# Starting the large on-chip buffers of a two-block transformer kernel at multiples of 128 bytes

## The chip, the cores and the metric

The kernel runs on one core of a Trainium2 chip. The metric is the device time of one execution in microseconds. Unless a sentence names the profiled execution, a time is the median over several executions.

## What is computed

The reference is two blocks, one after the other, on 256 tokens of width 1024, all in 32-bit floats.

```
first block (16 meta tokens are put ahead: 272 tokens)
    h = h + token_mixer(h)            # retention and mLSTM, both directions, 4 heads each
    h = h + expert_choice_ffn(h)      # 16 experts of width 2816, each takes its 34 best tokens
    h = rmsnorm(h)
second block, layers 0 and 1
    x = x + rmsnorm(mixer(rmsnorm(x)))          # layer 0: attention and convolution, layer 1: gated linear recurrence
    x = x + rmsnorm(cross_attention(x, memory)) # 256 memory rows
    x = x + rmsnorm(swiglu(rmsnorm(x)))         # width 2816
```

## The kernel before

Everything that stays on the chip lies in a handful of named buffers, allocated one behind the other in the order of the calls of `sb`, each 128 partitions by so many 32-bit columns:

- `weight_ring` (lines 148 ff., `W`), 22528 columns, takes the weights as they arrive from memory.
- `hT` is the stream, the running hidden state turned so that features lie on partitions. `squares` (`SQ`) is scratch of the same size.
- `arena` (`Z`), 25096 columns, is carved up by `z(...)` into the working tiles of each stage: the mixer's heads, the gathered tokens `xs` and hidden rows of the experts, the keys and values of the memory, and in the second block the normed input (`input_high`, `input_low`), the outputs of attention (`mixed_low`) and the hidden rows of the feed-forward layers (`hidden_high_a`, `hidden_high_b`).
- `rstd`, `vec_cols`, `gate_w`, `router_w` and `small` hold per-feature and per-token columns.

`rounded(name, over, at, cols)` (line 159) lays a second name over a part of a buffer, at `BASE[over] + 4 * at` bytes. It is how the tiles with names of their own come about: `weights_ring` over the first 20480 columns of `weight_ring`, `mixed_high` and `mixer_high_a` over the columns behind them, `hidden_low_b` over `hT`, and most others over `arena`.

The three long stages, in order of time:

1. The first mixer, to some 200 us.
2. The experts, from some 200 to 1500 us. Each of the 16 experts streams three weight matrices (gate, up, down: 2816 KB a transfer, four transfers a matrix) through eight slots of the ring. The tokens of an expert, 64 columns wide and held in the arena, are the stationary side of a matmul and the weights in the ring are the moving side (line 1250 for gate and up, line 1328 for down). Between them TensorE projects the memory rows to keys and values (line 1217), from weights which eight transfers of 2048 KB bring into the arena (line 588).
3. The second block, from some 1520 us. Its weights come in chunks of 1024 KB. ScalarE rounds each chunk to its high part (line 2141), VectorE takes the low part (line 2854), and a product is three passes: high times high, low times high, high times low (`three_passes`, and `token_part` for the first two chunks after a norm). For the input projections the stationary side is a piece of the weights and the moving side 256 columns of `input_high` or `input_low` (line 1369), except in `token_part` (line 1400), where the two change sides. For the output projections 512 columns of weights move and the stationary side is a 128-column piece of `mixed_high`, `mixed_low`, `hidden_high_a` and so on (also line 1369). Each of the two feed-forward layers has 22 input chunks of 48 matmuls.

The order of instructions on every engine is written out by hand and does not depend on where a buffer lies.

Of the kernel before, what the change touches and what calls it, by code (L numbers as in the profile page):

```python
# [22 lines left out]
KT = D // P  # L23
SEQ = 256
META = 16
T = META + SEQ
# [8 lines left out]
ARENA = 25096  # L35
# [91 lines left out]
def build(nc, t, out):  # L127

    with ExitStack() as ctx:
        BASE = {}  # L130

        def sb(name, cols, dt=F32):
            made = ctx.enter_context(nc.sbuf_tensor(name, [P, cols], dt))
            BASE[name] = nc.sbuf_base - 4 * cols
            return made
# [3 lines left out]
        def S(name):  # L139
            if name not in sems:  # L140
                sems[name] = ctx.enter_context(nc.semaphore(name))
            return sems[name]
# [2 lines left out]


        W = sb("weight_ring", SLOTS * SLOT)
        ident = sb("ident", P)
        ones = sb("ones", P)
        hT = sb("hT", KT * T)  # L150
        SQ = sb("squares", KT * T)
        RSTD = sb("rstd", T)
        VC = sb("vec_cols", 256)
        GW = sb("gate_w", KT * 16)
        RW = sb("router_w", KT * 16)
        small = sb("small", 192)
        Z = sb("arena", ARENA)

        def rounded(name, over, at, cols):

# [3 lines left out]
        def vec(name, i):  # L164
            tile, at, n = VEC_AT[name]
            return VC[:, tile * P + at + i:tile * P + at + i + 1]

        def vec_cols(name, n):
            tile, at, _ = VEC_AT[name]
            return VC[:, tile * P + at:tile * P + at + n]  # L170

        cursor = [0]

        def z(cols, at=None):
            if at is None:
                at = cursor[0]
                cursor[0] += cols
            assert at + cols <= ARENA, (at, cols)
            return Z[:, at:at + cols]

        def tiles(ap, n):
            return ap.rearrange("p (t n) -> p t n", t=n)
# [26 lines left out]
        mvT, moT, rkT, rqT, rvT, rgT = (z(H * T) for _ in range(6))  # L209
        rk_rq = Z[:, cursor[0] - 4 * H * T:cursor[0] - 2 * H * T]  # L210
        mv, rv = z(TT * 512), z(TT * 512)
        xtok = Z[:, cursor[0] - 2 * TT * 512:cursor[0]]
        DEC = z(H * TT * T)
        dist_fwd, dist_bwd = z(256 + T), z(256 + T)
        dist_both = Z[:, cursor[0] - 2 * (256 + T):cursor[0]]
        bar_fwd, bar_bwd = z(T), z(384)
# [25 lines left out]
        floors = tiles(QKP[:, 0:8 * T], 8)  # L242
        head_denom, head_square = SQ[:, 1632:1632 + T], SQ[:, 1632 + T:1632 + 2 * T]
        ret_squares = QKP[:, 0:H * T]
# [20 lines left out]
        mm = z(2 * KT * 256, 12288)  # L265
        mem_gains = VC[:, 192:208]
        utok = z(TT * D, 16384)
# [19 lines left out]
        logitsT, affW, picked, running, vals = (z(n, o + T * i) for i, n in enumerate((T, T, T, T, 40)))  # L287
        ys = SQ[:, 0:512]
        Se = SQ[:, 512:768]
        xs_tok = SQ[:, 768:1280]  # L290
        htok = hT[:, 0:2 * D]
# [16 lines left out]
        cu = hT[:, 1024:1024 + 4 * 258]  # L308
        fox_e = [SQ[:, 0:384], SQ[:, 384:768]]
        fox_pt = [SQ[:, 768:1152], SQ[:, 1152:1536]]  # L310
        frow, frow2, frow3 = YG[:, 0:256], YG[:, 256:512], YG[:, 512:768]
# [52 lines left out]
        def landed(s):  # L364
            return S(f"ring_landed{s}")
# [88 lines left out]
        def raw_slot(k):  # L454
            return W[:, (k % CSLOTS) * CSLOT:(k % CSLOTS) * CSLOT + SLOT]

        def second_half(k):
            return W[:, (k % CSLOTS) * CSLOT + SLOT:(k % CSLOTS + 1) * CSLOT]

# [56 lines left out]
        def _(sp):  # L516
# [7 lines left out]
            def stab_load(n):  # L524
                r = 4 * (n % 2) + n // 2
                sp.dma_start(stabs(n), unit_rows[r:r + 1].to_broadcast([P, T]))                  .then_inc(S("stab_landed" if n < 3 else "late_stab_landed"), 16)

            for k, (name, c) in enumerate(A_CHUNKS):
# [21 lines left out]
                if k == 15:  # L550
                    sp.wait_ge(S("pool_mixer"), H * TT)
                    sp.wait_ge(S("rot_out"), 2 * H)
                    for n in range(3, 8):
                        stab_load(n)
            sp.dma_start(tiles(RW[:], KT), t["w_router"][0].rearrange("(t p) n -> p t n", p=P))\
              .then_inc(S("router_w_landed"), 16)
# [7 lines left out]
            def expert_slot(s):  # L564
                return W[:, s * DFF:(s + 1) * DFF]

# [5 lines left out]
            def pair_slot(g):  # L572
                return W[:, 2 * g * DFF:2 * (g + 1) * DFF]

# [15 lines left out]
            def last_down_load():  # L590
# [3 lines left out]
                mid = (ESLOTS - 1) * DFF  # L594
                sp.dma_start(W[:, 2 * g * DFF:mid], src[:, 2 * g * DFF:mid]).then_inc(landed(g), 16)
                sp.dma_start(W[:, mid:LAST_ROWS], src[:, mid:LAST_ROWS]).then_inc(landed(ESLOTS - 1), 16)
                sp.dma_start(W[:, LAST_ROWS:FT * D], src[:, LAST_ROWS:FT * D]).then_inc(S("apart_landed"), 16)
# [201 lines left out]
        def _(pe):  # L799
# [282 lines left out]
            def router(group):  # L1082
# [3 lines left out]
                for i in group:  # L1086
                    g = i % 4
                    at = EXP * (i - 1 if g == 3 else i)
                    last = pe.matmul(bank[4][32 * g:32 * g + 32, 0:T], RW[:, at:at + 2 * EXP], stream3[:, i, :],
                                     start=(i < 4), stop=(i >= 4), skip_group_check=True)  # L1090
# [644 lines left out]
        def _(act):  # L1735
            steps = [0]

            def after(ins):

                steps[0] += 1  # L1740
                ins.then_inc(S("act_step"), 1)
                act.wait_ge(S("act_step"), steps[0])
# [295 lines left out]
            for e in range(EXP):  # L2038
# [6 lines left out]
                if e == 0:  # L2045
                    act.wait_ge(S("hidT_ready"), 1)
                    take_slots(0)
                    act.wait_ge(S("norm_sum"), 2)
                    after(act.activation(RSTD[:, 0:256], bank[7][:, 0:256], ACT.Ln, bias=eps, scale=1.0 / D))
                    act.activation(RSTD[:, 0:256], RSTD[:, 0:256], ACT.Exp, scale=-0.5).then_inc(S("norm_rstd"), 1)  # L2050
                if e + 1 < EXP:
# [368 lines left out]
        def _(dve):  # L2420
            steps = [0]

            def after(ins):

                steps[0] += 1
                ins.then_inc(S("dve_step"), 1)
                dve.wait_ge(S("dve_step"), steps[0])
# [34 lines left out]
            for j, n in enumerate(VEC_COUNT):  # L2462
                last = dve.tensor_copy(VC[:, P * j:P * j + n], bank[7][:, T + P * j:T + P * j + n])
            last.then_inc(S("small_ready"), 1)
# [17 lines left out]
            dve.memset(qkp[:, :, PAD + T:2 * PAD + T], 0.0).then_inc(S("small_ready"), 1)  # L2482
            dve.tensor_scalar(half_a, VC[:, B_A_AT:B_A_AT + 8], 0.5, None, ALU.mult)
            dve.tensor_scalar(half_i, VC[:, B_A_AT + 8:B_A_AT + 16], 0.5, None, ALU.mult).then_inc(S("small_ready"), 1)
            lam = VC[:, LAM_AT:LAM_AT + 8]
# [231 lines left out]
            gains = vec_cols("ffn_norm_g", KT).rearrange("p (t a) -> p t a", a=1).to_broadcast([P, KT, 16])  # L2717
            dve.tensor_tensor(tiles(RW[:], KT), tiles(RW[:], KT), gains, ALU.mult).then_inc(S("router_gain"), 1)
            after(dve.tensor_tensor(logit_rows, ident[:, 0:EXP], ident[:, 32:32 + EXP], ALU.add))
# [94 lines left out]
            for e in range(EXP):  # L2814
# [14 lines left out]
                if e == 0:  # L2829
                    dve.wait_ge(S("norm_rstd"), 1)  # L2830
                    m_T = tiles(mT, KT)
                    for L in range(2):
                        normed = tiles(mm[:, 2048 * L:2048 * L + 2048], KT)
                        for i in range(KT):
                            dve.scalar_tensor_tensor(out=normed[:, i, :], in0=m_T[:, i, :], scalar=mem_gains[:, 8 * L + i:8 * L + i + 1],
                                                     in1=RSTD[:, 0:256], op0=ALU.mult, op1=ALU.mult).then_inc(S("norm_out"), 1)
                dve.wait_ge(S("up_used"), 8 * e + 8)
# [439 lines left out]
```

## Time and profile before

| | |
|---|---|
| median of 3 executions | 2224.63 us (2223.53 to 2227.73) |
| the profiled execution | 2228.88 us, of which the span of instructions is 2227.1 us |
| granted TensorE clock, mean | 0.987 |
| TensorE matmul busy | 2106.0 us (95%) |
| TensorE weight load busy | 1307.8 us (59%) |
| VectorE busy | 770.7 us (35%) |
| ScalarE busy | 634.4 us (28%) |
| moved by DMA | 725.21 MB |

A matmul is issued before the one ahead of it has drained, so the busy time of TensorE counts overlapping intervals once, and the duration of one matmul is longer than the distance between two. Where the rate of TensorE matters, the distance between the starts of two groups in the timeline is what counts.

### The profile page before, as it was taken

How to read it: one execution, taken by the hardware profiler on the slowest of the kernel's cores; microseconds unless marked ns; L12 is line 12 of the kernel's file. 1: busy time of each engine (PE TensorE's matmuls, PEld its weight loads, DVE VectorE, ACT ScalarE, POOL GpSimd, SP SyncE). 2: the span in 40 equal slices, each digit the busy share in tenths (PEclk: the TensorE clock that was granted, in tenths of full speed). 3: DMA queues.
4: the chain of work that ended last, by engine and by line, in shares of the span. 5: the costliest groups of instructions: out<-in, count | busy, mean ns of one | idle time of the engine just before them, and what ended most of it. 6: DMA issues, size and time to landing. Idle time of an engine off the chain costs nothing.

```text
span 2227.1 us, 27225 instructions
## 1 busy us (share of the span) xinstructions
PE 2106.0 (95%) x12048; PEld 1307.8 (59%) x12048; DVE 770.7 (35%) x1105; ACT 634.4 (28%) x1008; POOL 43.2 (2%) x74
## 2 busy tenths in 40 slices
PE   9999999899898999899889889989999999999999
PEld 9987443333333443333333333427888998988997
DVE  8983211011010111011011011116765564876553
ACT  6664100000000000000000000005565444865442
POOL 3201000000000000000000000000000000000000
PEclk9999999999999999999999999999999999999999
DMA  8529999999999999999999999997444656544553
GB/s 238 173 83 384 419 430 428 430 427 432 427 431 429 430 429 429 429 428 430 429 430 429 429 429 430 416 428 246 148 164 151 215 190 204 173 157 149 197 190 114
DMA packets 145952, 725.21 MB, mean 326 GB/s; under 512 B 8614, under 2 KB 106330, under 8 KB 119466
## 3 DMA queue, kind: packets, MB, share of 16 engines
q1 hardware_dynamic: 144648, 721.47, 80.7%
q8 instruction: 95, 1.56, 0.3%
q0 software_dynamic: 640, 1.37, 0.2%
q10 hardware_dynamic: 546, 0.63, 0.1%
q14 instruction: 23, 0.19, 0.0%
HBM read 722.38 MB, written 1.07 MB: 325 GB/s over the span
## 4 chain that ended last, share of the span: by engine, by line
PE 60%; DMA 28%; DVE 7%; ACT 4%; issue 1%; DVEq 0%; ACTq 0%
PE bank L1369 22%; PE bank L1250 17%; DMA weight_ring<-in_w_down_dram 12%; DMA weight_ring<-in_w_up_dram 11%; PE bank L1328 7%; DMA weight_ring<-in_w_gate_dram 5%; PE bank L1217 5%; PE bank L1400 2%; DVE weights_ring L2447 1%; PE bank L1067 1%; DVE arena L2507 1%; ACT squares L2070 1%; PE bank L1181 1%; PE bank L1586 1%; PE bank L1609 1%
## 5 line engine op out<-in xcount | busy, mean ns | idle before, releaser
L1250 PE MATMUL bank<-weight_ring,arena 128*64 128x506 f32 x3024 | 631.1, 562 | 50.6 <-DMA weight_ring<-in_w_up_dram 40.1
L1250 PEld LDWEIGHTS bank<-weight_ring,arena 128*64 128x64 f32 x3024 | 217.8, 134 | 447.2 <-issue 362.3
L1328 PE MATMUL bank<-weight_ring,arena 128*64 128x512 f32 x1408 | 336.8, 631 | 48.1 <-DMA weight_ring<-in_w_down_dram 48.1
L2854 DVE TENSOR_TENSOR weights_ring<-weight_ring,weights_ring 128x2048 fp32r<-128x2048 f32 x110 | 249.8, 2289 | 126.9 <-ACT weights_ring L2141 126.6
L1328 PEld LDWEIGHTS bank<-weight_ring,arena 128*64 128x64 f32 x1408 | 103.0, 143 | 264.2 <-issue 195.9
L1369 PE MATMUL bank<-input_high,weights_ring 128*128 128x256 f32 x1920 | 245.6, 280 | 0.8 <-issue 0.8
L1369 PEld LDWEIGHTS bank<-input_high,weights_ring 128*128 128x128 f32 x1920 | 231.9, 188 | 2.9 <-issue 2.5
L2141 ACT ACTIVATE weights_ring<-weight_ring 128x2048 fp32r<-128x2048 f32 x109 | 205.7, 1908 | 59.9 <-DMA weight_ring<-in_w_ffn_down_dram 40.7
L2811 DVE TENSOR_TENSOR arena<-arena,bank 128x512 f32<-128x512 f32 x48 | 33.0, 687 | 529.8 <-PE bank L1217 529.8
L2042 ACT ACTIVATE arena<-bank 128x506 f32<-128x506 f32 (+1 forms) x48 | 23.5, 563 | 394.5 <-PE bank L1250 394.5
L1369 PE MATMUL bank<-input_low,weights_ring 128*128 128x256 f32 x960 | 130.9, 278 | 0.0
L1217 PE MATMUL bank<-arena 128*128 128x256 f32 x512 | 127.6, 392 | 0.0
L2062 ACT ACTIVATE squares<-bank 128x512 f32<-128x512 f32 x16 | 9.6, 597 | 396.9 <-PE bank L1328 396.9
L1217 PEld LDWEIGHTS bank<-arena 128*128 128x128 f32 x512 | 92.0, 189 | 52.0 <-issue 42.0
L1369 PEld LDWEIGHTS bank<-input_low,weights_ring 128*128 128x128 f32 x960 | 120.0, 188 | 0.0
L2017 ACT ACTIVATE squares<-bank 128x512 f32<-128x512 f32 x15 | 9.0, 597 | 360.6 <-PE bank L1181 360.6
L2800 DVE TENSOR_TENSOR hT<-hT,bank 128x512 f32<-128x512 f32 x60 | 38.5, 683 | 196.3 <-PE bank L1267 196.3
L1369 PE MATMUL bank<-weights_ring,mixed_high 128*128 128x512 f32 x320 | 94.0, 399 | 1.4 <-DVE weights_ring L2854 1.4
L2809 DVE COPY arena<-bank 128x512 f32<-128x512 f32 x16 | 11.1, 691 | 199.8 <-PE bank L1217 199.8
L1369 PE MATMUL bank<-weights_ring,hidden_high_a 128*128 128x512 f32 x256 | 70.4, 395 | 0.0
L1369 PEld LDWEIGHTS bank<-weights_ring,mixed_high 128*128 128x128 f32 x320 | 59.4, 188 | 15.0 <-issue 2.0
L2820 DVE SCALAR_TENSOR_TENSOR arena<-arena,bank 128x506 f32<-128x506 f32 (+1 forms) x48 | 28.0, 638 | 104.0 <-ACT arena L2042 104.0
(425 smaller groups left out, 2075.9 us busy)
## 6 DMA issues: line engine op xcount, KB each, us to landing
weight_ring<-in_w_down_dram SPq DMA_DIRECT2D x63, 2816.0 KB, 21.8
weight_ring<-in_w_up_dram SPq DMA_DIRECT2D x61, 2816.0 KB, 19.4
weight_ring<-in_w_gate_dram SPq DMA_DIRECT2D x60, 2816.0 KB, 18.9
weight_ring<-in_w_ffn_gu_dram SPq DMA_DIRECT2D x44, 1024.0 KB, 5.1
weight_ring<-in_w_ffn_down_dram SPq DMA_DIRECT2D x22, 1024.0 KB, 4.8
weight_ring<-in_w_in_dram SPq DMA_DIRECT2D x16, 1024.0 KB, 6.2
arena<-in_w_xkv_dram SPq DMA_DIRECT2D x8, 2048.0 KB, 23.7
weight_ring<-in_ab_w_in_dram SPq DMA_DIRECT2D x12, 1024.0 KB, 7.7
```

The costliest lines, as they stand in the source:

```text
L1067: last = pe.matmul(bank[pj.entries[A_OUT[n]][0]][:, 0:T], (high, low, high)[part][:, i, c], mix_low[:, T * i:T * i + T] if part == 2 else ...
L1217: last = pe.matmul(bank[7][:, 256 * a:256 * a + 256], w, x, start=(i == 0), stop=(i == 1))
L1250: last = pe.matmul(bank[first_bank + c][MPAD * half:MPAD * half + MPAD, 0:(hi - lo) * HF], xs3[:, s, :], w[:, lo:hi, HF * half:HF * half + ...
L1328: last = pe.matmul(bank[6][MPAD * half:MPAD * half + MPAD, :], hidT[:, at:at + MPAD], W[:, j * D + 512 * half:j * D + 512 * half + 512], s ...
L1369: last = pe.matmul(dst, w, y, start=start and n == 0, stop=stop and n == len(todo) - 1, skip_group_check=check)
L1400: last = pe.matmul(dst[:, 256 * t:256 * t + 256], x[:, i, tok], w[:, i, :], start=(n == 0 and i == 0), stop=(n == 2 and i == KT - 1))
L2042: act.activation(th[:, HF * lo:HF * hi], bank[c][:, 0:HF * (hi - lo)], ACT.Tanh, scale=0.5)\
L2141: act.activation(high_slot(k), raw_slot(k), ACT.Copy).then_inc(S("weights_high"), 1)
L2800: dve.tensor_tensor(rows, rows, bank[6 + n % 2][:], ALU.add).then_inc(S("scatter_taken"), 1)
L2811: ins = dve.tensor_tensor(dst, dst, bank[7][:], ALU.add)
L2820: dve.scalar_tensor_tensor(out=v, in0=v, scalar=1.0, in1=bank[c][:, 0:HF * (hi - lo)], op0=ALU.add, op1=ALU.mult)\
L2854: dve.tensor_tensor(low_slot(k), raw_slot(k), high_slot(k), ALU.subtract).then_inc(S("weights_low"), 1)
```

## The change

Eleven calls of `sb` are put in another order. The sizes, the instructions, and their order on every engine (1752 rows of TensorE, 725 of VectorE, 791 of ScalarE, 74 of GpSimd and 126 of SyncE, loops counted once) are the same before and after. Only addresses differ.

```
         W = sb("weight_ring", SLOTS * SLOT)
+        hT = sb("hT", KT * T)
+        SQ = sb("squares", KT * T)
+        VC = sb("vec_cols", 256)
         ident = sb("ident", P)
         ones = sb("ones", P)
-        hT = sb("hT", KT * T)
-        SQ = sb("squares", KT * T)
-        RSTD = sb("rstd", T)
-        VC = sb("vec_cols", 256)
         GW = sb("gate_w", KT * 16)
         RW = sb("router_w", KT * 16)
+        Z = sb("arena", ARENA)
+        RSTD = sb("rstd", T)
         small = sb("small", 192)
-        Z = sb("arena", ARENA)
```

The first of them starts 16512 bytes into a partition, and the sizes give the rest. The last two columns are the remainder of the start by 128.

| buffer | start before | start after | before, mod 128 | after, mod 128 |
|---|---|---|---|---|
| weight_ring | 16512 | 16512 | 0 | 0 |
| ident | 106624 | 125056 | 0 | 0 |
| ones | 107136 | 125568 | 0 | 0 |
| hT (the stream) | 107648 | 106624 | 0 | 0 |
| squares | 116352 | 115328 | 0 | 0 |
| rstd | 125056 | 227488 | 0 | 32 |
| vec_cols | 126144 | 124032 | 64 | 0 |
| gate_w | 127168 | 126080 | 64 | 0 |
| router_w | 127680 | 126592 | 64 | 0 |
| small | 128192 | 228576 | 64 | 96 |
| arena | 128960 | 127104 | 64 | 0 |

So the stream and the squares start at a multiple of 128 bytes in both versions. What gets there is the arena, with the three small tables `vec_cols`, `gate_w` and `router_w`, and `rstd` leaves it. By 256 bytes the arena's remainder goes from 192 to 128. The ring's, the stream's and the squares' is 128 in both.

## Rows read from the trace of the kernel before

**Rows 1.** The page: what the chain that ended last is made of, by engine.

```profile
PE 60%; DMA 28%; DVE 7%; ACT 4%; issue 1%; DVEq 0%; ACTq 0%
```

**Rows 2.** Busy time by window: experts, second block. Then PEclk, DMA share, GB/s.

```profile
600.00:1200.00 600.00, 553.23 (x2607) 221.54 (x2603) 71.87 (x131) 53.38 (x86) 0.00 (x0) 0.97 1.00 429
1520.00:2227.00 707.00, 692.79 (x4842) 636.22 (x4840) 440.24 (x469) 380.03 (x542) 1.04 (x1) 1.00 0.52 173
```

**Rows 3.** DMA issues whose target is the arena: count, KB each, us to landing.

```profile
arena<-in_w_xkv_dram SPq DMA_DIRECT2D x8, 2048.0 KB, 23.7
arena<-in_w_up_dram SPq DMA_DIRECT2D x1, 4224.0 KB, 16.1
```

**Rows 4.** Windows with a load into the arena (issued at 1297.2) and without.

```profile
1300.00:1350.00 50.00, 40.76 (x205) 14.88 (x205) 5.27 (x11) 2.73 (x6) 0.00 (x0) 1.00 1.00 429
...
1450.00:1490.00 40.00, 32.24 (x152) 10.61 (x152) 6.17 (x11) 2.75 (x4) 0.00 (x0) 1.00 1.00 431
```

**Rows 5.** Groups by line, VectorE and ScalarE: arena or aligned buffer as an operand.

```profile
L2800 DVE TENSOR_TENSOR hT<-hT,bank 128x512 f32<-128x512 f32 x60 | 38.5, 683 | 196.3 <-PE bank L1267 196.3
...
L2811 DVE TENSOR_TENSOR arena<-arena,bank 128x512 f32<-128x512 f32 x48 | 33.0, 687 | 529.8 <-PE bank L1217 529.8
...
L2070 ACT ACTIVATE squares<-arena 128x512 f32<-128x512 f32 x20 | 12.6, 632 | 12.3 <-DVE arena L2888 12.0
...
L2311 ACT ACTIVATE hidden_high_a<-squares 128x512 fp32r<-128x512 f32 x16 | 10.1, 633 | 83.0 <-DVE squares L3148 83.0
```

**Rows 6.** Weight loads by line: names are moving side, stationary side.

```profile
L1369 PEld LDWEIGHTS bank<-input_high,weights_ring 128*128 128x128 f32 x1920 | 231.9, 188 | 2.9 <-issue 2.5
...
L1369 PEld LDWEIGHTS bank<-input_low,weights_ring 128*128 128x128 f32 x960 | 120.0, 188 | 0.0
...
L1400 PEld LDWEIGHTS bank<-weights_ring,input_high 128*128 128x128 f32 x384 | 46.8, 188 | 6.1 <-DVE weights_ring L2854 2.9 <-ACT input_high L2111 1.8 <-issue 0.4
...
L1400 PEld LDWEIGHTS bank<-weights_ring,input_low 128*128 128x128 f32 x192 | 23.8, 188 | 0.0
```

**Rows 7.** Timeline of TensorE, first feed-forward layer: start us, us, group.

```profile
1716.24 1.07 PE L1369 MATMUL bank<-input_low,weights_ring 128*128 128x256 f32 x8
1717.14 1.98 PE L1369 MATMUL bank<-input_high,weights_ring 128*128 128x256 f32 x16
1718.96 1.07 PE L1369 MATMUL bank<-input_low,weights_ring 128*128 128x256 f32 x8
```

**Rows 8.** Timeline of TensorE, second feed-forward layer.

```profile
2054.55 1.10 PE L1369 MATMUL bank<-input_low,weights_ring 128*128 128x256 f32 x8
2055.49 2.04 PE L1369 MATMUL bank<-input_high,weights_ring 128*128 128x256 f32 x16
2057.38 1.10 PE L1369 MATMUL bank<-input_low,weights_ring 128*128 128x256 f32 x8
```

**Rows 9.** Timeline: `token_part` after the first attention.

```profile
1632.96 1.98 PE L1400 MATMUL bank<-weights_ring,input_high 128*128 128x256 f32 x16
1634.78 1.07 PE L1400 MATMUL bank<-weights_ring,input_low 128*128 128x256 f32 x8
1635.68 0.50 PE L1400 MATMUL bank<-weights_ring,input_high 128*128 128x256 f32 x3
```

**Rows 10.** Timeline: the same code, 8 us later.

```profile
1643.17 1.11 PE L1400 MATMUL bank<-weights_ring,input_low 128*128 128x256 f32 x8
1644.11 2.05 PE L1400 MATMUL bank<-weights_ring,input_high 128*128 128x256 f32 x16
1645.99 1.11 PE L1400 MATMUL bank<-weights_ring,input_low 128*128 128x256 f32 x8
```

**Rows 11.** Timeline: output projection of attention, one stationary side in three in the arena.

```profile
1613.36 1.09 PE L1369 MATMUL bank<-weights_ring,mixed_high 128*128 128x512 f32 x4
...
1617.52 1.08 PE L1369 MATMUL bank<-weights_ring,mixed_high 128*128 128x512 f32 x4
```

**Rows 12.** Timeline: down projection, every stationary side in the arena.

```profile
2190.31 1.10 PE L1369 MATMUL bank<-weights_ring,hidden_high_a 128*128 128x512 f32 x4
...
2194.51 1.10 PE L1369 MATMUL bank<-weights_ring,hidden_high_a 128*128 128x512 f32 x4
```

## The prediction

> **What bounds the kernel now.** I read the chain that ended last first, then the windows of the long stages, then single groups for the cost of an operand that starts 64 bytes off. The chain is TensorE for 60% and DMA for 28%; VectorE and ScalarE hold 7% and 4% [rows 1]. The windows say where each counts. In the experts the DMA engines are busy for the whole time and move 429 GB/s, while TensorE has idle time left (553 of 600 us busy) [rows 2]. The weights that pass through the ring set the length of that stage, and the ring does not move. In the second block it is the other way round: TensorE is busy for 693 of 707 us at the full granted clock, with DMA at 0.52 [rows 2]. So the change can only act by making the transfers of the experts' stage faster or slower, or by changing the distance between two matmuls of the second block, or by way of the 11% of the chain that is VectorE and ScalarE.
>
> **The change, part by part.** No instruction, wait or transfer is added, removed or moved. What changes is the start of operands: the arena goes from 64 bytes off a multiple of 128 to none, three small tables too, `rstd` and `small` end up 32 and 96 bytes off. The stream and the squares were already there. The trace never shows one operation at both places, so I bound each effect by pairs of rows that differ in the buffer alone.
>
> *VectorE and ScalarE.* The same 128x512 addition takes 683 ns on `hT` (0 off) and 687 ns on the arena (64 off). The same ScalarE pass takes 632 ns when it reads the arena and 633 when it reads the squares [rows 5]. So at most 4 ns for a VectorE instruction. VectorE's 7% of the chain is 156 us, at some 600 ns each 260 instructions, which makes 1.0 us if all of them gained 4 ns. ScalarE gives nothing. I take 0, since 4 ns is also what two lines on like operands differ by, and keep a gain of 1.0 us as the bound. The same 4 ns bounds a loss on the instructions that read `rstd` and `small`, which are fewer. Call it 0 to +0.5 us.
>
> *Transfers.* Into the arena go eight loads of 2048 KB and one of 4224 KB, with smaller ones some 23 MB in the experts' stage [rows 3], at 429 GB/s 54 us of transfer. A window that begins with such a load moves 429 GB/s, one without moves 431 [rows 4]. If the 2 GB/s were the cost of the 64 bytes, eight such windows of 50 us at 0.5% would give 1.9 us. That is more than 23 MB can plausibly lose, and 2 GB/s is also what windows of 50 us scatter by, so I take 0 and keep −1.9 us as the end.
>
> The Trainium skill, "DMA: Bandwidth & Descriptors", section "How a descriptor splits into AXI transactions", says that what counts for a descriptor is whether it starts at a multiple of 256 bytes, and that the bytes between that boundary and the start cost beats of 32 bytes. By that rule 128 is not enough: the arena is off the boundary before (by 192) and after (by 128), and only two beats in the 514 or so of a 16 KB row go, which I estimate at 0.2 us over all loads. The trace agrees in so far as the ring, also 128 off the boundary in both versions, already moves 429 GB/s.
>
> *Weight loads of TensorE.* 128 columns take 188 ns whether the stationary side is a piece of the ring (0 off, line 1369) or of `input_high` in the arena (64 off, line 1400) [rows 6]. Nothing to gain there.
>
> *The distance between matmuls of 256 columns.* Here is what I would look at longest. In the first feed-forward layer 24 matmuls take 2.72 us, in the second 2.83 us [rows 7, 8]. It is the same code on the same tiles. A buffer's start can't be the reason, since `input_high` lies at the same place both times. `token_part`, with the ring moving and the arena stationary, shows the same two rhythms, 2.72 us and 2.82 us, within 13 us of each other [rows 9, 10]. So there are two rhythms, 0.11 us apart in 24 matmuls, TensorE falls into one or the other behind an interruption and stays in it, and neither side's alignment selects it. There are 1920 + 960 + 384 + 192 = 3456 such matmuls [rows 6], or 144 groups of 24, of which 44 in each feed-forward layer. I take no change.
>
> *The distance between matmuls of 512 columns.* In the output projection of attention, where one stationary side in three lies in the arena, three turns of six matmuls take 4.16 us, or 1.387 us each. In the down projection, where all do, 4.20 us or 1.400 [rows 11, 12]. If that is due to the 64 bytes, each third costs 0.0067 us in six matmuls. The two down projections have 88 such groups (32 with two thirds in the arena, 32 with three, 24 with two, so 208 thirds) and the four output projections 64 groups with one third. That is 272 × 0.0067 = 1.8 us. The equal weight loads speak against it, and 0.04 us in three turns is four steps of the timeline's last digit. I take half, −0.9 us.
>
> The sum is 0 + 0 + 0 + 0 − 0.9, and the profiled execution would go from 2228.88 to 2228.0 us. That execution lies 4.3 us above the median of the three, which is about what one feed-forward layer in the longer rhythm costs (44 × 0.11 = 4.8 us). The median would go from 2224.6 to 2223.7 us. Three runs spread over 4.2 us (0.19%), so a difference of under 0.2% (4.4 us) is about what a measurement of this kernel can't tell from none.
>
> **The rivals.**
> *Faster: the 64 bytes hold TensorE in the longer rhythm.* Then the aligned arena puts every 256-column group at 2.72 us. The second feed-forward layer gives back 44 × 0.11 = 4.8 us. Of the 56 groups outside the two layers I take half to be long, 28 × 0.11 = 3.1 us. With the 1.8 us above this comes to −9.7 us, or 2214.9, and without it to 2216.7. For it: the longer rhythm is there and costs something. Against it: the first layer ran the short one at the old start [rows 7].
>
> The Trainium skill, "TensorE: Matmul & The Clock Gate", section "Back-to-back issue gap", gives columns over 2.4 GHz plus 2.5 ns as the distance between isolated matmuls. For 256 columns that is 109 ns, under both rhythms (113 and 118 ns). Were the excess the price of the start, the estimate from that page would be some 22 us off, or 2203. The page itself says that with a weight load to each matmul other distances hold, and line 1400, whose moving side is aligned already, shows no 109.
>
> *Slower: the change flips the first feed-forward layer into the longer rhythm.* The arena moves by 1856 bytes and the squares by 1024, so other addresses meet in time, and the arrival of TensorE at line 1369 shifts. It decides from the point where the whole layer runs at 2.83 us: 44 × 0.11 = +4.8 us, or 2229.4. With the groups outside the layers as well it is +7.9 us, or 2232.5. For it: the rhythm changes behind small interruptions, and two of them are within 13 us [rows 9, 10]. Against it: nothing ties it to an address, and it may differ from one execution to the next anyway, in which case the medians show it on both sides.
>
> *The experts' stage gets slower or faster by contention between transfers and TensorE's reads.* DMA share is 1.00 at 429 GB/s with TensorE reading all the time [rows 2], for slots at eight different starts. I see no room for it. It would have to change by 0.3% of 1300 us to show.
>
> **How the numbers follow.** No change that can be told: 0.75, at 2219.5 to 2229, its likeliest value 2223.7. The longer rhythm cured, or the other gains together (1.0 + 1.9 + 1.8 = 4.7 us, 2219.9): 0.14. The longer rhythm caught: 0.10. Contention: 0.01. The range of 2217.5 to 2230 goes from nearly the full cure to the flip of one layer and leaves out under 2 in 10. Chances: faster 0.14, same 0.75, slower 0.11.
>
> **What the profile of the changed kernel would show.** Experts: DMA share 1.00 and 429 GB/s between 600 and 1200 us, TensorE still with idle time. VectorE and ScalarE groups on the arena within 4 ns of before, weight loads at 188 ns. Down projection: 1.38 us for six matmuls if the 64 bytes cost something, 1.40 if not. Feed-forward layers: 2.72 or 2.83 us for 24 matmuls, in either layer. I would be wrong if both layers and both kinds of projection showed 2.72 in every execution (first rival), if they showed 2.83 in both (second), if a distance under 2.72 appeared, or if the experts' stage changed its length by over 3 us.

## The result and the profile after

The change makes the kernel slower, by some 0.3%.

| | median | executions | ratio, 95% interval |
|---|---|---|---|
| before | 2227.53 us (2223.53 to 2229.07) | 6 | |
| after | 2234.57 us (2234.24 to 2235.95) | 6 | 1.0032 (1.0018 to 1.0046) |

The profiled execution after took 2234.51 us, its span 2232.7 us. The span grew by 5.6 us. Five of the six executions after lie within 0.4 us, while those before spread over 5.5 us. The median before stood at 2224.63 us with the three executions that the prediction had, and at 2227.53 us with six.

The long stages first. The windows of the kernel after, with the columns of [rows 2]:

```profile
600.00:1200.00 600.00, 552.54 (x2611) 221.06 (x2613) 72.58 (x132) 52.42 (x85) 0.00 (x0) 0.98 1.00 429
1520.00:2227.00 707.00, 700.43 (x4836) 648.86 (x4833) 436.13 (x464) 378.21 (x535) 1.04 (x1) 1.00 0.52 171
```

The experts' stage is what it was, DMA share 1.00 and 429 GB/s. In the second block TensorE is busy for 700 of 707 us, up from 693, and at 2227 us it is not done. The granted clock of that stage is 1.00 before and after, so the clock is not what changed.

Where the time comes in is read from one kind of row, the transposes (line 1352) with which the second half of a norm begins. In the timeline of TensorE they begin as follows, first in the kernel before, ahead of the second block, the first feed-forward layer, the second block's layer 1, and the second feed-forward layer:

```profile
1520.71 1.32 PE L1352 MATMUL bank<-ident,arena 128*128 128x128 f32 x8 [0.56 <-DVE arena L2947]
...
1703.52 1.32 PE L1352 MATMUL bank<-ident,arena 128*128 128x128 f32 x8 [0.23 <-DVE arena L2898]
...
1888.62 1.32 PE L1352 MATMUL bank<-ident,arena 128*128 128x128 f32 x8 [0.17 <-DVE arena L2898]
...
2038.83 1.32 PE L1352 MATMUL bank<-ident,arena 128*128 128x128 f32 x8 [0.23 <-DVE arena L2898]
```

and in the kernel after:

```profile
1519.03 1.32 PE L1352 MATMUL bank<-ident,arena 128*128 128x128 f32 x8 [0.57 <-DVE arena L2947]
...
1703.01 1.32 PE L1352 MATMUL bank<-ident,arena 128*128 128x128 f32 x8
...
1893.46 1.32 PE L1352 MATMUL bank<-ident,arena 128*128 128x128 f32 x8
...
2043.83 1.32 PE L1352 MATMUL bank<-ident,arena 128*128 128x128 f32 x8
```

The kernel after is 1.7 us ahead at the start of the second block, 0.5 us ahead at the first feed-forward layer, 4.8 us behind when that layer is over, 5.0 behind at the second and 5.6 at the end. So the first feed-forward layer alone costs 5.3 us. Of the rest, 1.2 us come between the start of the block and that layer. The lead at the start of the block is no more than scatter: over the traces of all kernels here this row begins between 1519.0 and 1521.7 us, and in a second trace of the unchanged kernel before it begins 1.2 us earlier than in the first. TensorE waits for VectorE ahead of all four rows before, and after ahead of the first alone: at the other three TensorE now arrives later than the result that it used to wait for.

In that layer the timeline after shows the input projections like this (start, duration, group, as in [rows 7]):

```profile
1740.04 2.08 PE L1369 MATMUL bank<-input_high,weights_ring 128*128 128x256 f32 x16
1741.96 1.12 PE L1369 MATMUL bank<-input_low,weights_ring 128*128 128x256 f32 x8
1742.92 2.08 PE L1369 MATMUL bank<-input_high,weights_ring 128*128 128x256 f32 x16
```

24 matmuls take 2.88 us (1742.92 − 1740.04), 120 ns each. Before, it was 2.72 in this layer and 2.83 in the other [rows 7, 8]. Both layers are at 2.88 now. The down projection went the other way:

```profile
2189.95 1.07 PE L1369 MATMUL bank<-weights_ring,hidden_high_a 128*128 128x512 f32 x4
...
2192.68 1.07 PE L1369 MATMUL bank<-weights_ring,hidden_high_a 128*128 128x512 f32 x4
```

Two turns of six take 2.73 us here, and over the layer a turn takes 1.36 us on average (227 ns a matmul), where it was 1.40 [rows 12]. The two numbers give the stage times back. First layer: 44 × (2.88 − 2.72) = +7.0 and 44 × (1.36 − 1.40) = −1.8, together +5.2 (5.3 seen). Second layer: 44 × (2.88 − 2.83) = +2.2 and −1.8, together +0.4 (0.6 seen).

The output projections of attention gain too. Before, they took 1.387 us for six [rows 11], and after

```profile
1614.29 1.07 PE L1369 MATMUL bank<-weights_ring,mixed_high 128*128 128x512 f32 x4
...
1617.01 1.07 PE L1369 MATMUL bank<-weights_ring,mixed_high 128*128 128x512 f32 x4
```

two turns take 2.72 us, 1.36 each. Their 64 groups give back some 1.7 us. It is more than eaten up by the 256-column groups outside the two feed-forward layers, most of which went from 2.83 to 2.88 us: from the start of the second block on, the stretches outside these layers grew by 1.3 us.

VectorE and ScalarE did not change. Of the groups of [rows 5], the addition on the arena takes 688 ns (687), the one on `hT` 684 (683), and ScalarE's pass over the arena 633 (632):

```profile
L2800 DVE TENSOR_TENSOR hT<-hT,bank 128x512 f32<-128x512 f32 x60 | 38.6, 684 | 199.1 <-PE bank L1267 199.1
...
L2811 DVE TENSOR_TENSOR arena<-arena,bank 128x512 f32<-128x512 f32 x48 | 33.0, 688 | 529.2 <-PE bank L1217 529.2
...
L2070 ACT ACTIVATE squares<-arena 128x512 f32<-128x512 f32 x20 | 12.7, 633 | 12.5 <-DVE arena L2888 12.2
```

But the weight loads of the 256-column matmuls, 188 ns in [rows 6], are longer:

```profile
L1369 PEld LDWEIGHTS bank<-input_high,weights_ring 128*128 128x128 f32 x1920 | 239.0, 192 | 2.5 <-issue 2.3
```

That stationary side is in the ring, which did not move. Only the moving side next to it did. So a load's duration can depend on where the other operand lies. It does not in every kind: the loads for matmuls of 512 columns take 188 ns in both kernels.

### The profile page after: what moved, and what is told of

The parts are those of the page before. It is cut to its first block, busy times and chain, and to the rows that moved or that the text cites. A ratio compares the mean times of both kernels' runs of the same rounds, so it can differ in the third digit from the quotient of the medians.

```text
span 2232.7 us, 27225 instructions
## 1 busy us (share of the span) xinstructions
PE 2109.3 (94%) x12048; PEld 1320.0 (59%) x12048; DVE 770.2 (34%) x1105; ACT 634.8 (28%) x1008; POOL 43.2 (2%) x74
## 3 DMA queue, kind: packets, MB, share of 16 engines
q0 software_dynamic: 640, 1.37, 0.2%
## 4 chain that ended last, share of the span: by engine, by line
PE 62%; DMA 28%; DVE 6%; ACT 3%; issue 1%; DVEq 0%; ACTq 0%
PE bank L1369 22%; PE bank L1250 17%; DMA weight_ring<-in_w_up_dram 10%; DMA weight_ring<-in_w_down_dram 10%; DMA weight_ring<-in_w_gate_dram 7%; PE bank L1328 6%; PE bank L1217 5%; PE bank L1400 3%; DVE weights_ring L2447 1%; PE bank L1181 1%; PE bank L1067 1%; DVE arena L2507 1%; PE bank L1586 1%; PE bank L1609 1%; PE bank L1352 1%
## 5 line engine op out<-in xcount | busy, mean ns | idle before, releaser
L1328 PE MATMUL bank<-weight_ring,arena 128*64 128x512 f32 x1408 | 329.2, 619 | 50.3 <-DMA weight_ring<-in_w_down_dram 50.1
L1369 PE MATMUL bank<-input_high,weights_ring 128*128 128x256 f32 x1920 | 252.8, 284 | 0.5 <-issue 0.4
L1369 PEld LDWEIGHTS bank<-input_high,weights_ring 128*128 128x128 f32 x1920 | 239.0, 192 | 2.5 <-issue 2.3
```

Of the source, the lines that this page charges most:

```text
L1328: last = pe.matmul(bank[6][MPAD * half:MPAD * half + MPAD, :], hidT[:, at:at + MPAD], W[:, j * D + 512 * half:j * D + 512 * half + 512], s ...
L1369: last = pe.matmul(dst, w, y, start=start and n == 0, stop=stop and n == len(todo) - 1, skip_group_check=check)
```

## The experiments

In all of them the instructions are those of the kernel. Only addresses change, and nothing is left out. The table is in terms of one number, d: a tile's start minus the ring's start, in bytes modulo 256 (so −64 is the same as 192). It is +64 for the arena before and 0 after. "256" is the time of 24 matmuls of 256 columns in the first feed-forward layer, "512" that of six of 512 columns in the down projection where both halves of the hidden rows are in the arena, `hidden_high_a` and `mixed_low`. The kernel before ran beside each set on the same chip, and its own median moves with the set. The end of this section says what is known of that.

| kernel | d of inputs | d of outputs, hidden rows | 256, us | 512, us | median, us | before beside it |
|---|---|---|---|---|---|---|
| before | +64 | +64 | 2.72 or 2.83 | 1.40 | | 2227.53 |
| after | 0 | 0 | 2.88 | 1.36 | 2234.57 | 2227.53 |
| arena aligned alone | 0 | 0 | 2.88 | 1.36 | 2235.24 | 2232.53 |
| new order, arena 64 off | −64 | −64 | 2.72 | 1.37 | 2222.68 | 2232.53 |
| inputs 64 off | +64 | 128 | 2.82 | 1.39 | 2232.38 | 2232.53 |
| outputs 64 off | 0 | +64 | 2.88 | 1.40 | 2238.61 | 2232.53 |
| everything 64 off | 0 | 0 | 2.88 | 1.36 | 2235.48 | 2228.36 |
| ring 64 off, arena aligned | −64 | −64 | 2.72 | 1.37 | 2222.00 | 2228.36 |
| inputs 64 below | −64 | 0 | 2.72 | 1.36 | 2219.90 | 2228.36 |

The last of these beats both kernels. Rows three to six of the table were run on one chip, the last three on another. Kernels that agree in both d agree in their medians to 1 us, whichever the chip.

### Is it the arena, or the rest of the new order?

*Arena aligned alone* is the kernel before with `vec_cols` at 240 columns, its last 16 not being used:

```
-        VC = sb("vec_cols", 256)
+        VC = sb("vec_cols", 240)
```

> The old order of the buffers, with vec_cols cut from 256 to 240 columns (none of the last 16 is used), so that everything behind it, the arena above all, starts 64 bytes earlier and at a multiple of 128; the stream, the squares, rstd stay where they were. Theory A (the arena's remainder by 128 does it): as the changed kernel, 2234.6 us, with 120 ns between the matmuls of 256 columns in both feed-forward layers and 227 ns between those of 512. Theory B (the new places of rstd and small, or the shift of the stream and the squares by 1024 bytes do it): as before, 2227.5 us, with 113 or 118 ns and 233 ns.

Measured: 2235.24 us (2234.28 to 2236.78), and the two rhythms of the kernel after. The order of the buffers, the stream, the squares and the place of `rstd` are as before. So moving the arena by 64 bytes, with the small tables behind `vec_cols` that move along, is enough, and theory B falls. From its timeline:

```profile
1740.16 2.08 PE L1369 MATMUL bank<-input_high,weights_ring 128*128 128x256 f32 x16
1742.08 1.12 PE L1369 MATMUL bank<-input_low,weights_ring 128*128 128x256 f32 x8
1743.04 2.08 PE L1369 MATMUL bank<-input_high,weights_ring 128*128 128x256 f32 x16
```

*New order, arena 64 off* is the same cut made in the kernel after.

> The new order with vec_cols at 240 columns, so that the arena is 64 bytes off again and all else is in the new order. Theory A: as before, 2223 to 2229 us, with 113 or 118 ns and 233 ns. Theory B: 2234.6 us.

Measured: 2222.68 us (2221.11 to 2223.41), ratio to before 0.9956 (0.9941 to 0.9971). The alignment theory got the direction, and missed the size: this is faster than the kernel before, not like it. 24 matmuls take 2.72 us in both layers, as its timeline shows for the first (1742.06 to 1744.78), and six of 512 columns 1.37 us (2190.66 to 2192.03):

```profile
1742.06 1.98 PE L1369 MATMUL bank<-input_high,weights_ring 128*128 128x256 f32 x16
1743.87 1.07 PE L1369 MATMUL bank<-input_low,weights_ring 128*128 128x256 f32 x8
1744.78 1.41 PE L1369 MATMUL bank<-input_high,weights_ring 128*128 128x256 f32 x11
```

```profile
2190.66 1.08 PE L1369 MATMUL bank<-weights_ring,hidden_high_a 128*128 128x512 f32 x4
2191.58 0.62 PE L1369 MATMUL bank<-weights_ring,mixed_low 128*128 128x512 f32 x2
2192.03 1.08 PE L1369 MATMUL bank<-weights_ring,hidden_high_a 128*128 128x512 f32 x4
```

Both places are 64 past a multiple of 128. By 256 they differ: 192 before, 64 here, with the ring at 128. "Aligned to 128 or not" can't be the whole rule.

### Which tiles?

*Inputs 64 off* and *outputs 64 off* move tiles inside the arena of the kernel after. The first is

```
-        x_high = rounded("input_high", "arena", 14336, 2 * D)
-        x_low = rounded("input_low", "arena", 16384, 2 * D)
-        y_low = rounded("mixed_low", "arena", 18432, 2 * D)
+        x_high = rounded("input_high", "arena", 14336 + 16, 2 * D)
+        x_low = rounded("input_low", "arena", 16384 + 16, 2 * D)
+        y_low = rounded("mixed_low", "arena", 18432 + 32, 2 * D)
...
-        WORK = 20480
+        WORK = 20480 + 32
```

> The changed kernel with the two tiles of the normed input (input_high, input_low) 16 columns later in the arena, 64 bytes off, and mixed_low and all tiles behind it 32 columns later, still aligned. Theory A by parts (the 256-column matmuls lose by alignment, the 512-column ones gain, each by its own arena tile): 256 columns back at 113 or 118 ns, 512 columns stay at 227 ns; 144 groups of 24 win 0.05 to 0.16 us each, so 2234.6 minus 7 to 23 us, my estimate 2221 us, faster than both kernels. If the remainder of another tile matters: 2234.6 us.

and the second leaves the inputs where they are and adds 16 to the last two.

> The changed kernel with mixed_low and all tiles behind it in the arena 64 bytes off, the normed input aligned. Theory A by parts: 120 ns for 256 columns stays, 512 columns go back to 230 to 236 ns where the stationary side is in those tiles; that costs 3 to 5 us: 2238 to 2239 us, slower than both kernels. If only the input tiles matter: 2234.6 us.

Measured: 2232.38 us (2231.38 to 2235.97) for the first, and 2238.61 us (2237.62 to 2239.66) for the second, ratio 1.0028 (1.0017 to 1.0039). The second came as expected, 2.88 and 1.40 us. The first missed by 11 us. The inputs at +64 fell into the 2.82 us rhythm in both layers, and the hidden rows, which I had moved by 128 bytes and called aligned, went to 1.39 us: they are 128 from the ring modulo 256, and that is not the same as 0. So the two kinds of matmul can be set apart by tile, and again 256 bytes count. From the timeline of the first:

```profile
1739.82 2.05 PE L1369 MATMUL bank<-input_high,weights_ring 128*128 128x256 f32 x16
1741.70 1.10 PE L1369 MATMUL bank<-input_low,weights_ring 128*128 128x256 f32 x8
1742.64 2.04 PE L1369 MATMUL bank<-input_high,weights_ring 128*128 128x256 f32 x16
```

The second holds a control of its own. Its down projections take the last chunks of the hidden rows from `hidden_high_b`, which starts at the arena's start and was not moved. First a turn on the moved `hidden_high_a`, then one on `hidden_high_b`, in the same layer:

```profile
1869.70 1.10 PE L1369 MATMUL bank<-weights_ring,hidden_high_a 128*128 128x512 f32 x4
...
1871.10 1.10 PE L1369 MATMUL bank<-weights_ring,hidden_high_a 128*128 128x512 f32 x4
...
1876.62 1.07 PE L1369 MATMUL bank<-weights_ring,hidden_high_b 128*128 128x512 f32 x4
...
1877.98 1.07 PE L1369 MATMUL bank<-weights_ring,hidden_high_b 128*128 128x512 f32 x4
```

On the moved tile six matmuls take 1.40 us, on the one left in place 1.36.

### A tile's own start, or its distance from the ring?

*Everything 64 off* puts `rstd` (1088 bytes, 64 past a multiple of 128) ahead of the ring:

```
+        RSTD = sb("rstd", T)
         W = sb("weight_ring", SLOTS * SLOT)
...
         Z = sb("arena", ARENA)
-        RSTD = sb("rstd", T)
```

> The changed kernel with rstd moved to the front, so that the ring, the stream, the squares, the tables and the arena all start 64 bytes off a multiple of 128 (192 past one of 256). Theory R (what counts is the distance between the arena's start and the ring's, here 0 modulo 256 as in the changed kernel): 120 ns for 256 columns and 227 ns for 512, 2234 to 2235 us. Theory S (what counts is each tile's own start): rhythms of before, 113 or 118 ns and 230 to 236 ns, so 2223 to 2233 us.

*Ring 64 off, arena aligned* has `vec_cols` at 240 columns as well.

> rstd in front and vec_cols at 240 columns: the ring, the stream and the squares are 192 past a multiple of 256, the arena 128 past one. The arena is as far below the ring (64 bytes, modulo 256) as in the new order with the arena 64 off. Theory R: 113 ns for 256 columns throughout and 230 ns for 512, 2221 to 2224 us. Theory S with the arena's own start as the cause: 120 ns and 227 ns, 2234.6 us.

Measured: 2235.48 us (2234.42 to 2237.21), ratio 1.0035 (1.0023 to 1.0046), and 2222.00 us (2221.20 to 2224.00), ratio 0.9974 (0.9963 to 0.9984). This decides it. With none of the large buffers aligned the kernel runs like the one after. With the arena aligned exactly as there and the ring moved, it runs like the fast one. From their timelines, first everything 64 off, then the ring 64 off:

```profile
1740.57 2.08 PE L1369 MATMUL bank<-input_high,weights_ring 128*128 128x256 f32 x16
1742.49 1.12 PE L1369 MATMUL bank<-input_low,weights_ring 128*128 128x256 f32 x8
1743.45 2.08 PE L1369 MATMUL bank<-input_high,weights_ring 128*128 128x256 f32 x16
```

```profile
1742.43 1.98 PE L1369 MATMUL bank<-input_high,weights_ring 128*128 128x256 f32 x16
1744.24 1.07 PE L1369 MATMUL bank<-input_low,weights_ring 128*128 128x256 f32 x8
1745.15 1.07 PE L1369 MATMUL bank<-input_high,weights_ring 128*128 128x256 f32 x8
```

The first has 2.88 us between its two rows of 16, the second 2.72.

Nor does it take more than 256 bytes to state the distance: modulo 512 the arena lies 256 from the ring in *arena aligned alone* and 0 in the kernel after, and both show 2.88 us.

### The best of both, and the distances between

*Inputs 64 below* is the kernel after with 48 columns added to the two inputs and 64 to `mixed_low` and `WORK`.

> The changed kernel with input_high and input_low 48 columns later in the arena (192 bytes, so 64 below the ring's start modulo 256) and mixed_low and all tiles behind it 64 columns later (256 bytes, so 0 from the ring's). Theory R: the short rhythm of the 256-column matmuls, 113 ns, as in the new order with the arena 64 off, and the 227 ns of the changed kernel for 512 columns. 152 groups of six gain 0.02 us against that variant: 2219 to 2221 us, the fastest so far. If the two tiles can't be set apart: 2223 us or more.

Measured: 2219.90 us (2219.57 to 2220.64), ratio 0.9958 (0.9946 to 0.9970) to before, within what was expected. Its timeline has the short rhythm of 256 columns and the short one of 512 (2189.98 to 2191.34, 1.36 us):

```profile
1742.50 1.98 PE L1369 MATMUL bank<-input_high,weights_ring 128*128 128x256 f32 x16
1744.31 1.07 PE L1369 MATMUL bank<-input_low,weights_ring 128*128 128x256 f32 x8
1745.22 1.98 PE L1369 MATMUL bank<-input_high,weights_ring 128*128 128x256 f32 x16
```

The short rhythm of 256 columns holds in both feed-forward layers, but not everywhere. In the input projections of the two mixers, at the same d, the same trace shows the longer one, 2.83 us:

```profile
1544.13 2.05 PE L1369 MATMUL bank<-input_high,weights_ring 128*128 128x256 f32 x16
...
1546.96 2.05 PE L1369 MATMUL bank<-input_high,weights_ring 128*128 128x256 f32 x16
```

The other two traces at −64 show the same in all but one group each. So −64 too has two rhythms, and in the layers and the mixers it is the place that goes with one or the other. What picks it was not tested. At 0 the mixers' projections show 2.88 like the layers.

Then the turns of 512 columns of *inputs 64 below*:

```profile
2189.98 1.07 PE L1369 MATMUL bank<-weights_ring,hidden_high_a 128*128 128x512 f32 x4
2190.88 0.62 PE L1369 MATMUL bank<-weights_ring,mixed_low 128*128 128x512 f32 x2
2191.34 1.07 PE L1369 MATMUL bank<-weights_ring,hidden_high_a 128*128 128x512 f32 x4
```

Four more only change the 48 to 56, 8, 32 and 40 columns.

> As the variant with the inputs 64 below the ring (modulo 256), but 32 below. If the cost falls off in steps of 64 bytes: 120 ns as at 0, or 113 ns as at -64, and about 2233 or 2220 us. If it goes with the distance: between the two, some 117 ns.

> The inputs 32 above the ring modulo 256, all else aligned. At 0 the distance between matmuls of 256 columns is 120 ns, at +64 it is 118 or 113. Expected: one of these or a value between, so 2225 to 2233 us.

> The inputs 128 from the ring modulo 256, so at a multiple of 256 themselves. If the relation repeats every 128 bytes: 120 ns as at 0, 2233 us. If it repeats every 256 bytes, a rhythm of its own: any of 113, 118 or 120 ns. The tiles behind mixed_low lay 128 off in an earlier variant and showed 233 ns for 512 columns where 0 off shows 227, so I expect another value than at 0.

> The inputs 96 below the ring modulo 256. If distance below the ring is what helps, 113 ns or less, 2219 to 2220 us. If 64 is a place of its own: 117 to 120 ns, 2227 to 2233 us.

The kernel before had a median of 2232.53 us beside them. "256" is from the timeline, as above.

| d of the inputs | −96 | −64 | −32 | 0 | +32 | +64 | 128 |
|---|---|---|---|---|---|---|---|
| 256, us for 24 | 2.82 | 2.72 | 2.84 | 2.88 | 2.80 | 2.72 or 2.83 | 2.85 |
| median, us | 2230.08 | 2219.90 | 2230.17 | 2234.57 | 2228.38 | | 2232.23 |

The column 0 is that of the kernel after, whose other tiles lie at 0 like those of the variants. +64 is that of the kernel before. Its median is left out, since other tiles differ there. Each of the four was inside its wide expectation, and −96 came out as the second of its two cases, no better than −64. The relation is neither a step nor a slope: 64 bytes below is a place of its own, and 32 bytes to either side of it cost 0.10 to 0.12 us in 24 matmuls, or about 10 us in the median. The variant at −64 was run on another chip than the other four, so the 10 us are between sets. The 0.10 to 0.12 us are between traces, and 88 groups of them in the two layers give 9 to 11 us.

### The spread of the kernel before

> The kernel before, unchanged, for a second trace. If the feed-forward layers fall into the short or the long rhythm by chance or by chip, this trace shows another pairing than short in the first layer and long in the second: long in both would give some 5 us more than the first trace, 2232 to 2234 us, and short in both 5 us less. If the rhythm is fixed by the program: short in the first, long in the second, 2228 us.

Measured: 2231.7 us in its one execution, unchanged in every instruction and address, with the longer rhythm in both layers. Its timeline in the first feed-forward layer, where [rows 7] had 2.72 us:

```profile
1741.41 2.04 PE L1369 MATMUL bank<-input_high,weights_ring 128*128 128x256 f32 x16
1743.30 1.10 PE L1369 MATMUL bank<-input_low,weights_ring 128*128 128x256 f32 x8
1744.24 2.05 PE L1369 MATMUL bank<-input_high,weights_ring 128*128 128x256 f32 x16
```

So at d = +64 one program falls into either rhythm, layer by layer, from one execution to the next. The 19 executions of the kernel before beside the variant above show it in their times: 2 at 2222.8 to 2223.1, 10 at 2226.2 to 2228.8, 7 at 2231.7 to 2232.8 us. The steps are near the 4.8 us of one layer (44 × 0.11). The upper two groups each have a trace (2231.7 and 2228.9 us). That the lowest is short in both layers is inferred: it was not traced in this kernel. It would also explain why the median before differs between sets: in the two with 2232.53 us, 19 of 23 and 25 of 29 executions are above 2230 us, in this one 7 of 19. Each of the three sets had a chip of its own, so whether the chip has a part in the choice is not known. The ratio of *arena aligned alone*, whose time is that of the kernel after, is only 1.0015 (1.0006 to 1.0025) because the kernel before was slower beside it. At d = 0 and −64 the executions of a kernel lie within 1 to 3 us.

## Why the prediction was wrong

It forecast no change, 2223.7 us, with a range to 2230. It came out at 2234.6, on the side to which it had given 0.11. Of the 10.9 us between, about 3 are the level of the kernel before, taken from three executions (2224.6 for 2227.5), and about 8 are the change itself, +7.0 where −0.9 was forecast.

- **The experts' stage, VectorE, ScalarE.** Right. 429 GB/s as before, durations within 1 ns. The gains of up to 1.9 and 1.0 us that were kept as bounds are not seen: the second block starts 1.7 us earlier, which is within the scatter of that row.
- **Weight loads.** "Nothing to gain there" rested on two groups with 188 ns. Both had one operand in the ring and one in the arena, so both had the same distance, +64 or −64. They could not show what 0 does. It gives 192 ns on line 1369.
- **Matmuls of 256 columns, the step that failed.** The prediction saw two rhythms at the same addresses and concluded that "neither side's alignment selects it". What the rows bear out is less: at this one distance there are two rhythms. That one address allows two says that something besides the address acts, not that the address does not. At distance 0, which the trace of before does not contain in these matmuls, there is a third, 2.88 us, longer than both. The term taken as 0 was +7.0 us in the first layer and +2.2 in the second.
- **Matmuls of 512 columns.** The mechanism was seen, and the sign was right: the stationary sides in the arena cost time at +64. The term was −0.9 with −1.8 us as its end. Measured, the down projections gain 2 × 1.8 us, −3.6 in all, more than the end, and the output projections of attention some 1.7 more. The cost does not go in equal parts by thirds: the straight line through one third and three thirds had its foot at 1.380 us, while 1.36 is what 0 gives. The 0.04 us that I halved as too near the last digit were real.
- **The rivals.** The faster one, that alignment cures the longer rhythm, has the right place and the wrong sign. The slower one, that other addresses bring a longer rhythm, names what happened more nearly than the forecast did. But it knew only 2.83 us, so its price stopped at 2229.4 for one layer and 2232.5 for all. It was given 0.10 because "nothing ties it to an address". The 2.88 us of distance 0 is tied to the addresses. The choice between 2.72 and 2.83 at +64 is not, as far as was seen.
- **The median before.** The guess that the 4.3 us between the profiled execution and the median were one layer's rhythm fits the groups of the 19 executions, but 2224.6 us itself lies between two of them, and no execution of that kind was traced.

The Trainium skill, "TensorE: Matmul & The Clock Gate", section "Step-by-step: what each phase is for", says that TensorE reads the moving and the stationary side through two independent ports and that loading the next weights takes no read bandwidth from the running matmul. Taken alone, that gives no reason for the distance between the two tiles to matter. These runs show that it does: 24 matmuls take 2.72 us at −64 and 2.88 at 0, and moving both tiles by 64 bytes together leaves it at 2.88. Whether the two reads share anything inside the chip was not measured and stays open, as does what picks the rhythm at +64 and −64.

## What to carry to other kernels

Where TensorE streams pairs of weight load and matmul from rounded 32-bit tiles without a gap, the starts of the moving and the stationary tile belong together: try their distance modulo 256 bytes, per kind of matmul, before the alignment of either, since one shift of a common buffer can help one kind and hurt the other. A trace that holds one distance says nothing of others, and two rhythms at one address are a sign that TensorE is sensitive there, not that the address is harmless. When executions of one program fall into groups some microseconds apart, read the distance between matmuls in two traces before comparing medians.

## What was not expected of the hardware

The distance between 256-column matmuls of rounded 32-bit operands takes steady values that depend on the two start addresses: 113.3 ns (2.72 us for 24), 116.7 to 118.7, and 120.0 (2.88 us). At +64 and at −64 two of them occur in the same program. The order of merit differs for 512 columns, where 0 is best (1.36 us for six), then −64 (1.37 to 1.38). 128 (1.39) and +64 (1.40) come last, and their order holds for that kind of group alone: where the low part of the hidden rows is in the ring, +64 shows 1.39 and 128 1.40 to 1.41.
